# mLSTM block: the o and z projection slots cut into halves between the steps of the four heads, gating on VectorE, both token sets in one matmul

## The reference, cut to what matters

```python
xm, o_pre, z = split(hmod @ w_in, 3)              # 1024 -> 3 x 2048, latent and context tokens
xconv = silu(depthwise_conv3x3(xm) + conv_b)
q = xconv @ w_q ; k = (xconv @ w_k) * 512 ** -0.5 # per head, 4 heads of 512
v = xm
li, lf = gates(q, k, v)                           # per head and direction
# two directions r, context tokens first, their state carried into the latent tokens:
#   scores = (q k^T) * exp(decay of the forget gates + input gate - running maximum)
#   h_r    = scores v / max(|sum(scores)|, exp(-maximum))
hn = normalise(h_0 + h_1) * ln_w                  # mean and variance over the 512 of a head
y  = (sigmoid(o_pre) * hn + skip * xconv) * silu(z)
x  = x + g * (y @ w_out)                          # latent tokens only: o_pre, z, w_out see 256 tokens
```

## Time and profile before

| | |
|---|---|
| median of 3 runs | 1388.94 us (1386.91 to 1389.7) |
| the profiled execution | 1390.78 us, span 1388.9 us |
| mean granted TensorE clock | 0.961 of full speed |
| TensorE busy | 1269.3 us, 91% of the span |
| VectorE, ScalarE, GpSimd busy | 804.8, 577.3, 259.9 us |

### The profile page before, as it was taken

How to read it: one execution, slowest core, us unless ns; L and a number is a source line. 1 busy time by engine, 2 the same in 40 slices (tenths; PEclk the granted TensorE clock), 3 DMA queues, 4 the chain that set the end, 5 groups by cost and what they waited for, 6 DMA issues and landing times.

```text
span 1388.9 us, 23065 instructions
## 1 busy us (share of the span) xinstructions
PE 1269.3 (91%) x9496; PEld 1178.6 (85%) x9496; DVE 804.8 (58%) x1182; ACT 577.3 (42%) x874; POOL 259.9 (19%) x198
## 2 busy tenths in 40 slices
PE   5799999999976789899998998999989968999997
PEld 2699877779954579899998988999989957999996
DVE  2767844436446577654436676555456996555544
ACT  3332433334532313444235445444345555544433
POOL 1233300045430011000200040111001972111100
PEclk9799999999988899999999999999999989999999
DMA  9556211115530004455133534555543304355551
GB/s 390 219 211 265 98 61 61 61 61 182 182 121 1 0 31 168 158 183 184 48 122 124 185 146 145 185 182 183 184 152 122 122 31 152 124 183 182 183 190 47
DMA packets 27473, 195.56 MB, mean 141 GB/s; under 512 B 3192, under 2 KB 3328, under 8 KB 3968
## 3 DMA queue, kind: packets, MB, share of 16 engines
q1 hardware_dynamic: 26496, 191.90, 38.6%
q10 hardware_dynamic: 896, 2.50, 0.5%
HBM read 193.33 MB, written 1.05 MB: 140 GB/s over the span
## 4 chain that ended last, share of the span: by engine, by line
PE 79%; DVE 13%; ACT 4%; issue 1%; POOL 0%; ACTq 0%; DVEq 0%
PE ps L401 23%; PE ps L403 23%; PE ps L402 23%; PE ps L443 3%; PE ps L608 3%; DVE acc L1908 3%; DVE w_lo L1406 1%; PE ps L540 1%; DVE V L1647 1%; PE ps L458 1%; DVE xconv L1512 1%; DVE rstd L1717 1%; ACT w_hi L859 1%; DVE wexp L1650 1%; PE ps L596 1%
## 5 line engine op out<-in xcount | busy, mean ns | idle before, releaser
L1406 DVE TENSOR_TENSOR w_lo<-ring,w_hi 128x1024 fp32r<-128x1024 f32 x288 | 359.1, 1257 | 330.5 <-ACT w_hi L859 325.3
L859 ACT ACTIVATE w_hi<-ring 128x1024 fp32r<-128x1024 f32 x312 | 327.0, 1058 | 491.2 <-PE ps L403 412.0
L401 PE MATMUL ps<-x_hi,w_hi 128*128 128x256 f32 x1216 | 349.8, 288 | 20.2 <-DVE x_lo L1726 20.2
L402 PE MATMUL ps<-x_lo,w_hi 128*128 128x256 f32 x1216 | 348.6, 287 | 0.0
L403 PE MATMUL ps<-x_hi,w_lo 128*128 128x256 f32 x1216 | 348.4, 286 | 0.0
L401 PEld LDWEIGHTS ps<-x_hi,w_hi 128*128 128x128 f32 x1216 | 238.0, 196 | 22.5 <-issue 22.5
L402 PEld LDWEIGHTS ps<-x_lo,w_hi 128*128 128x128 f32 x1216 | 237.9, 196 | 0.0
L403 PEld LDWEIGHTS ps<-x_hi,w_lo 128*128 128x128 f32 x1216 | 237.7, 196 | 0.0
L401 PE MATMUL ps<-g_hi,w_hi 128*128 128x256 f32 x608 | 171.0, 281 | 2.5 <-POOL g_lo L1350 1.1
L403 PE MATMUL ps<-g_hi,w_lo 128*128 128x256 f32 x608 | 170.2, 280 | 0.0
L402 PE MATMUL ps<-g_lo,w_hi 128*128 128x256 f32 x608 | 169.4, 279 | 0.0
(11 more groups left out here) (299 smaller groups left out, 2157.7 us busy)
## 6 DMA issues: line engine op xcount, KB each, us to landing
ring<-in_weights SPq DMA_DIRECT2D x156, 1024.0 KB, 4.9
o_sb<-in_weights SPq DMA_DIRECT2D x10, 1024.0 KB, 6.5
z_sb<-in_weights SPq DMA_DIRECT2D x10, 1024.0 KB, 7.0
V<-in_weights SPq DMA_DIRECT2D x3, 1024.0 KB, 22.6
dft<-in_dft ACTq DMA_DIRECT2D x1, 1026.0 KB, 5.1
X<-in_x SPq DMA_DIRECT2D x1, 1024.0 KB, 4.9
ctx_room<-in_ctx SPq DMA_DIRECT2D x1, 1024.0 KB, 7.7
xconv<-in_weights SPq DMA_DIRECT2D x1, 1024.0 KB, 27.2
```

What stands on the lines that cost most here:

```text
L401: mm(dst, w_h, x_h, start=start, stop=False, skip_group_check=True)
L402: mm(dst, w_h, x_l, start=False, stop=False, skip_group_check=True)
L859: do(w_hi[:, q % 2, part], ring[:, q % RING, part], ACT.Copy).then_inc(S("hi_ready"), 1)
L1406: v.tensor_tensor(w_lo[:, q % 2, part], ring[:, q % RING, part], w_hi[:, q % 2, part], ALU.subtract).then_inc(S("lo_ready"), 1)
```

## The change

1. **Both token sets side by side.** `hc` and `hl` become one tensor `h`, and each pair of `triple`s of 256 columns in `xm_slot` becomes one of 512 columns.
2. **The order.** The oz slots are reordered by head (`block_of`: o, o, z, z for every half head), and TensorE's list is written in halves of slots: 11 halves stand before the denominators of head 0 and six with each head, at fixed places; three mout halves are among those of head 3 and 13 behind it. Each head now completes before the next one's denominators. The oz slots use two PSUM banks instead of four. ScalarE's and VectorE's queues are rewritten to the same pattern.
3. **Gating.** GpSimd keeps only memsets here. `apply_z` on VectorE multiplies o and xconv by ln_w or skip and by z, in one instruction for each chunk of 128 channels (32 in all); `rest_of_y` moves to VectorE; the rounding of y moves from VectorE to ScalarE (`round_y`).
4. **Homes.** z has two buffers in free rows of `V` instead of a tensor; `wexp` no longer shares with `hl`; the remainder of y lies in rows of `V` whose head is done. `spread` reads 128 partitions, of which 124 are zero, instead of 4; GpSimd clears them first. The loads of the oz slots are written out one by one.

```diff
+    if STARTS["oz"] <= q < STARTS["mout"]:
+        t = q - STARTS["oz"]
+        q = STARTS["oz"] + 2 * (t // 4) + t % 2 + N_OZ // 2 * (t % 4 // 2)
...
-        hc, qk_hi, room = one_place("room", (P, KE, CTX), ("hc", (P, 2, KD, CTX), F32R),
-                                    ("qk_hi", (P, 2 * HC, TOK), F32R))
-
-        hl, wexp2 = one_place("wexp", (P, 2, 2, 4, SEQ), ("hl", (P, 2, KD, SEQ), F32R))
+        both_stack = ExitStack()
+        h = tensors(both_stack)("h", (P, 2, 2, KD, SEQ), F32R)
+        both_stack.close()
+        hc, hl = h[:, 0], h[:, 1]
+        qk_hi, room = one_place("room", (P, KE, CTX), ("qk_hi", (P, 2 * HC, TOK), F32R))
+        sa("hl_room", (P, KE, SEQ))
...
-        y_lo, qk_lo, z_sb = one_place("z_sb", (P, KE, SEQ), ("y_lo", (P, KE, SEQ), F32R),
-                                      ("qk_lo", (P, 2 * HC, TOK), F32R))
-        V = sa("V", (P, HC + KE, TOK))
+        ada_room, qk_lo, wexp2 = one_place("wexp", (P, 2, 2, 4, SEQ), ("ada_room", (P, KE, SEQ), F32),
+                                           ("qk_lo", (P, 2 * HC, TOK), F32R))
+        y_rest, V = one_place("V", (P, HC + KE, TOK), ("y_rest", (P, HC + KE, TOK), F32R))
...
+        z_sb = [V[:, KE + n, :].rearrange("p (b j) -> p b j", b=2) for n in range(2)]
+
+        def y_lo(c):
+
+            return y_rest[:, HC * (c // HC) + c % HC // 2, (c % 2) * SEQ:(c % 2 + 1) * SEQ]
...
-            load_rest(first_rest, STARTS["mout"])
+            load_rest(first_rest, STARTS["oz"])
+            for q in range(STARTS["oz"], STARTS["mout"]):
+                load(q)
...
-                            triple(ps[:, bank, 0:CTX], w, [hc[:, a, k, :] for a in range(2)], k == 0, False)
-                            last = triple(ps[:, bank, CTX:TOK], w, [hl[:, a, k, :] for a in range(2)], False,
-                                          k == KD - 1)
+                            last = triple(ps[:, bank, :].rearrange("p (t j) -> p t j", t=2), w,
+                                          [h[:, :, a, k, :] for a in range(2)], k == 0, k == KD - 1)
...
+            pe.wait_ge(S("v_moved"), 4 * HEADS)
             for g in range(4):
-                if g == 2:
-                    pe.wait_ge(S("scores_moved"), HEADS)
-                last = mm(ps[0:4, (6, 7, 4, 5)[g], :], gate_fold[:, 4 * g:4 * g + 4], gates, start=True, stop=True)
+                last = mm(ps[0:4, g, :], gate_fold[:, 4 * g:4 * g + 4], gates, start=True, stop=True)
...
+            def oz_half(t, half):
+
+                if half == 0 and t >= 2:
+                    pe.wait_ge(S("oz_moved"), t - 1)
+                pe.wait_ge(S("lo_ready"), 2 * (STARTS["oz"] + t) + half + 1)
+                for k in range(4 * half, 4 * half + 4):
+                    for b in range(2):
+                        last = triple(ps[:, 6 + t % 2, b * SEQ:(b + 1) * SEQ],
+                                      [w[:, t % 2, k, b * P:(b + 1) * P] for w in wide_tiles],
+                                      [hl[:, a, k, :] for a in range(2)], k == 0 and b == 0, k == KD - 1)
+                last.then_inc(S("slot_done") if half else S("half_used"), 1)
+
+            def mout_half(t, half):
+
+                c = 2 * t + half
+                if t == 0 and half == 0:
+                    pe.wait_ge(S("oz_moved"), N_OZ)
+                    pe.wait_ge(S("heads_moved"), HEADS - 1)
+                pe.wait_ge(S("lo_ready"), 2 * (STARTS["mout"] + t) + half + 1)
+                pe.wait_ge(S("y_ready"), c // HC + 1)
+                for m in range(KD):
+                    last = triple(acc[:, m, :], [w[:, t % 2, half, m * P:(m + 1) * P] for w in deep_tiles],
+                                  (y_hi[:, c, :], y_lo(c)), c == 0 and m % 2 == 0, half == 1)
+                    if t == N_MOUT - 1 and half == 1 and m in (1, 3, 5):
+                        last.then_inc(S("bank_summed"), 1)
+                last.then_inc(S("slot_done") if half else S("half_used"), 1)
+
+            def halves(a, z):
+
+                for n in range(a, z):
+                    if n < 2 * N_OZ:
+                        oz_half(n // 2, n % 2)
+                    else:
+                        mout_half((n - 2 * N_OZ) // 2, n % 2)
+
...
             def spread(hd):
 
                 if hd:
                     pe.wait_ge(S("diag_ready"), hd)
                     pe.wait_ge(S("wexp_ready"), hd)
-                sel = cc("select", hd * P, (hd + 1) * P)[0:HEADS]
-                mm(ps[:, 0, :], sel, grow(2)[:, 0], start=True, stop=True)
-                mm(ps[:, 1, :], sel, grow(3)[:, 0], start=True, stop=True).then_inc(S("spread_done"), 1)
+                else:
+                    pe.wait_ge(S("floor_ready"), 1)
...
+                sel = cc("select", hd * P, (hd + 1) * P)
+                mm(ps[:, 0, :], sel, room[:, 4:6, :], start=True, stop=True)
+                mm(ps[:, 1, :], sel, room[:, 6:8, :], start=True, stop=True).then_inc(S("spread_done"), 1)
...
+            halves(0, 7)
+            columns()
+            halves(7, 8)
+            spread(0)
+            halves(8, 11)
             for n in range(HEADS):
-                if n >= 1:
-                    denominators(n - 1)
-                spread(n)
-                if n >= 2:
-                    head_mean(n - 2)
-                if n >= 1:
-                    mix_values(n - 1)
-                if n >= 2:
-                    head_var(n - 2)
-
-            denominators(HEADS - 1)
-            head_mean(HEADS - 2)
-            out_slots(0, 1)
-            mix_values(HEADS - 1)
-            head_var(HEADS - 2)
-            out_slots(1, 2)
-            head_mean(HEADS - 1)
-            out_slots(2, 3)
-            head_var(HEADS - 1)
...
+                at = 11 + 6 * n
+                denominators(n)
+                halves(at, at + 3)
+                if n + 1 < HEADS:
+                    spread(n + 1)
+                mix_values(n)
+                halves(at + 3, at + 4)
+                head_mean(n)
+                halves(at + 4, at + 6)
+                head_var(n)
+            halves(11 + 6 * HEADS, 2 * (N_OZ + N_MOUT))
 
             def norm(name, centred, n=KD, weight=ones_d, src=X, sqs=sq):
...
+            def move_oz(t):
+
                 act.wait_ge(S("slot_done"), STARTS["oz"] + t + 1)
-                dst = (o_sb if t < 8 else z_sb)[:, 2 * (t % 8):2 * (t % 8) + 2, :]
-                do(dst, ps[:, u, :].rearrange("p (b j) -> p b j", b=2), ACT.Sigmoid if t < 8 else ACT.Silu)\
+                n = 2 * (t // 4) + t % 2
+                if t % 4 >= 2 and n >= 2:
+                    act.wait_ge(S("z_applied"), 4 * (n - 1))
+                dst = o_sb[:, 2 * n:2 * n + 2, :] if t % 4 < 2 else z_sb[n % 2]
+                do(dst, ps[:, 6 + t % 2, :].rearrange("p (b j) -> p b j", b=2), ACT.Sigmoid if t % 4 < 2 else ACT.Silu)\
                     .then_inc(S("oz_moved"), 1)
 
+            def next_slot(t):
+
                 hi(STARTS["oz"] + t + 2)
-                move_oz(t, t % 4)
-                if t == N_OZ // 2:
-                    act.wait_ge(S("m_ready"), 1)
-                    do(grow(3)[:, 0], grow(3)[:, 0], ACT.Exp, scale=-1.0).then_inc(S("floor_ready"), 1)
+                if t < N_OZ:
+                    move_oz(t)
 
...
+            def round_y(hd):
+
+                act.wait_ge(S("head_scaled"), hd + 1)
+                do(y_hi[:, HC * hd:HC * hd + HC, :], work(2 * (hd % 2)), ACT.Copy).then_inc(S("y_rounded"), 1)
+
+            for t in range(3):
+                next_slot(t)
+            act.wait_ge(S("m_ready"), 1)
+            do(grow(3)[:, 0], grow(3)[:, 0], ACT.Exp, scale=-1.0).then_inc(S("floor_ready"), 1)
+            next_slot(3)
+            weigh(0)
+            next_slot(4)
             for n in range(HEADS):
-                weigh(n)
...
+                next_slot(5 + 3 * n)
+                next_slot(6 + 3 * n)
+                if n + 1 < HEADS:
+                    weigh(n + 1)
+                move_values(n)
+                if n:
+                    round_y(n - 1)
+                squares(n)
+                next_slot(7 + 3 * n)
+                root(n)
+            next_slot(N_OZ + 1)
+            round_y(HEADS - 1)
...
+            pool.wait_ge(S("scores_done"), HEADS)
+            nc.gpsimd.memset(room[:, 4:8, :], 0.0).then_inc(S("spread_clear"), 1)
...
-            pool.wait_ge(S("slot_done"), STARTS["oz"])
-            pool.wait_ge(S("vec_ready"), 16)
...
-            for t in range(N_OZ // 2):
-                pool.wait_ge(S("oz_moved"), t + 1)
-                for c in (2 * t, 2 * t + 1):
-                    nc.gpsimd.tensor_scalar(o_sb[:, c, :], o_sb[:, c, :], vcol("ln_w", c), None, ALU.mult)\
-                        .then_inc(S("o_scaled"), 1)
-            for t in range(N_OZ // 2):
-                pool.wait_ge(S("oz_moved"), N_OZ // 2 + t + 1)
-                pool.wait_ge(S("o_scaled"), 2 * t + 2)
-                pool.wait_ge(S("skip_ready"), 2 * t + 2)
-                c = slice(2 * t, 2 * t + 2)
```

(77 more changed lines are left out.)

62 lines of the change are left out of this document (15 added, 47 removed).

## The result

| | before | changed |
|---|---|---|
| median | 1388.47 us (4 runs, 1386.91 to 1389.7) | 1341.9 us (4 runs, 1338.37 to 1343.18) |
| ratio, 95% interval | | 0.9657, 0.9643 to 0.9671 |
| profiled execution: span | 1388.9 us | 1339.9 us |
| granted TensorE clock | 0.961 | 0.971 |

The kernel became 46.6 us faster; 1337 was forecast, with 1331 to 1352 as the range. The page of the changed kernel answers the earlier trace rows: TensorE's share of the chain that ended last has grown from 79% to 82%, and VectorE's has shrunk from 13% to 10%.

The account below looks back on a forecast made before the run. TensorE bounds it, through idling and slow clock. The stage saves 48.8 us, with xm 52.6: from 1390.8 to 1338.2, 1.8 lower for the median, 1336.4, plus half a microsecond: 1337, range 1331 to 1352.

Parts of the forecast that it names:

- the stage, grow rows to the end of mout: Oz slots, heads and mout: 204.6 us of TensorE work plus 3.8 of waits, 208.4 instead of 257.2.
- waits in it: TensorE's remaining waits in the stage: 3.0 us in the first oz slots, up to 0.6 at head 0, 0.2 in mout.
- division to values: margin for heads 1 and 3: VectorE needs 8.4 us between denominators and values; TensorE has 10.4 of other work, 8.64 for the last head.
- values to mean: margin: Between values and mean ScalarE moves 1024 elements, about 1.1 us, under one half slot of 2.88: margin 1.6.
- merged matmul, to the grow rows: Xm slots 1 to 6: 288 pairs save 13.3 ns each, 3.8 us; bounds 0 and 4.5.
- rival 2: The clock doesn't recover: fine-grained waits keep TensorE at 1.2 GHz in the values, giving back 15 us, 1352; chance 0.06.
- VectorE as the bound: VectorE's list takes 20% longer than summed, a head 36.7 us instead of 32.8, 15.6 more in all, 1353; chance 0.15.
- The clock not recovering: TensorE stays at 1.2 GHz in the values because of fine-grained waits; 15 us back, 1352; chance 0.06.
- Queues locking: In-order queues: one late item stops slots and heads alike, half the stage's gain lost, 24 us, 1361; chance 0.04.
- slower: Scattered plain float32 matmuls bring the clock down for the slots too; all at half clock 1541; chance 0.02.
- no effect: Something else keeps the heads behind the oz slots, so the change doesn't do what it says; chance 0.01.
- the half microsecond that I had added: Allowance for small handovers, half a microsecond added to 1336.4 us to give 1337.

Follow-up runs that it names:

- lo_first: Changed kernel with VectorE's splits of oz slots 2 and 3 ahead of the first scan and of g; 1339.45 us.
- before_fillers: Kernel before, with 4, 4, 5 and 8 unused matmuls ahead of the wait of mix_values of heads 0 to 3; 1387.17 us, ratio 0.9987.
- two_triples: Changed kernel with the xm slots' pair as two matmuls of 256 columns again; 1342.47 us.
- four_rows: Changed kernel with the spread over 4 rows instead of 128, as in the kernel before; 1342.26 us.
- more_tables: Changed kernel with ScalarE loading the table of Sqrt behind the move of every oz slot from the fifth on; 1338.33 us.
- order_undone: Changed kernel with only the order undone: all oz slots, columns, then heads two deep, y's rounding on VectorE, its rest on GpSimd; 1386.71 us, ratio 0.9982.
- late_slack: Changed kernel with an unused 128x512 reciprocal on VectorE for heads 1 to 3, at the end of its list; 1341.82 us.
- late_division: Changed kernel with an unused 128x512 reciprocal on VectorE for heads 1 to 3, inside the division ahead of its two passes; 1349.62 us.
- mended: Changed kernel with splits of oz slots 2 and 3 first, unused matmuls in the norms and two ahead of the first qk_lo wait; 1328.37 us, ratio 0.9561.

## Why the prediction was right, point by point

The forecast was 4.9 us too low, 0.4% of the time, on the right side and by the mechanism named. What it had wrong is the merged matmul, counted whole to the end, and the clock behind TensorE's waits of about 2 us, which it put at nothing. Term by term:

| term | predicted | measured |
|---|---|---|
| the stage, grow rows to the end of mout | 208.4 us | 209.35 |
| waits in it | 3.8 | 2.6 |
| distance from head to head | 32.8 | 32.75 |
| VectorE's work for one head, with eight gating products | 30.6 | 29.7 (head 2) |
| VectorE busy in the stage | 165 | 158.4 |
| division to values: margin for heads 1 and 3 | 1.7 and 0 | 1.68 and 0.05 |
| values to mean: margin | 1.6 | 1.6 |
| table loads in the stage; ScalarE busy | 21 (8 and 13 more); 118 us | 23 (10 before, 13 more); 117.5 us |
| merged matmul, to the grow rows | 3.8 | 1.4 (3.1 in the traces in which the clock held) |
| the norm behind mout | unchanged | 1.8 longer |

- **The order** held in all its parts. The stage is 0.95 us over the sum although the waits are 1.2 less, so 2.15 us are something else. Behind the wait of 2.2 us, eighteen matmuls of oz slot 2 take 3.66 us (313.64 to 317.30) instead of 2.16, 1.5 us, which I had not counted; the last 0.65 is not placed. lo_first shows it: without that wait the stretch is at 1.00. But the same wait, 2.24 to 2.39 us, left the clock at 1.00 in four traces (the kernel before, before_fillers, two_triples, four_rows), and lowered it in seven. My argument against rival 2, that the clock was 1.00 in the oz run with its waits, rested on one of the four. VectorE's 29.7 are the 32.75 between the divisions of heads 2 and 3 less 3.04 of waiting. I had taken w_lo at 1.2 a half, where it is 2.27 for two in a row (415.80 to 418.07), and the four masks at 1.6 where they took 1.03. For head 1, with four gating products, it is 28.1. w_lo has lost its slow passes next to GpSimd, as expected; the group answers the earlier trace rows:

```profile
L1421 DVE TENSOR_TENSOR w_lo<-ring,w_hi 128x1024 fp32r<-128x1024 f32 x46 | 54.3, 1220 | 12.3 <-ACT w_hi L892 12.2
```

- **The merged matmul** is the term that failed. The slot became 0.60 us shorter (rows of the adaptive weights 12.97 us apart, 13.57 before), 12.5 ns a pair where I had 13.3. The Trainium skill, "TensorE: Matmul & The Clock Gate", section "Back-to-back issue gap", would have made it 2.5 ns by its gap of an isolated matmul; the trace does not agree. The step that failed is "slots 1 to 6 save 288 x 13.3 ns = 3.8 us" taken whole to the end, by way of "That run begins 3.8 us earlier and is no shorter". Two things took from it.

  First, VectorE. ScalarE's move behind slot 6 comes 3.65 us earlier after the mark (78.87 instead of 82.52), but VectorE's first split comes only 2.1 us earlier (82.03 instead of 84.13). Before, VectorE had stood idle for 4.50 us ahead of it. Now it is still in the convolution, whose last two passes take 5.12 us instead of 0.88, while GpSimd's two w_lo passes run. Before, and then now:

```profile
139.99 0.88 DVE L1521 SCALAR_TENSOR_TENSOR xconv<-V,vec,xconv  x2 [0.15 <-DVE xconv L1512]
145.36 3.31 DVE L1528 TENSOR_TENSOR xsplit<-xconv,xsplit 128x512 fp32r<-128x512 f32 x4 [4.50 <-ACT xsplit L953]
```

```profile
136.93 5.12 DVE L1536 SCALAR_TENSOR_TENSOR xconv<-V,vec,xconv  x2 [0.15 <-DVE xconv L1527]
141.98 2.48 DVE L1543 TENSOR_TENSOR xsplit<-xconv,xsplit 128x512 fp32r<-128x512 f32 x4
136.84 4.93 POOL L1338 TENSOR_TENSOR w_lo<-ring,w_hi 128x1024 fp32r<-128x1024 f32 x2 [7.62 <-ACT w_hi L892]
```

  That GpSimd's passes cause it is my reading of the times and was not tested by itself. Over six xm slots VectorE is busy 66.0 us of 77.8, where it was 58.0 of 81.5. The splits themselves are 0.9 us quicker, so q of head 0 is released 2.95 us earlier (107.08 instead of 110.03 us after the mark). two_triples, with the old matmuls, has the first split at 84.12 and the release at 110.01 again.

  Second, the clock. TensorE gained 4.2 us over seven slots and waits 2.2 us for the release instead of 0.9. Behind that wait the stretch of the qk slots takes 12.77 us at a clock of 0.87. In the kernel before it took 11.19 at 1.00:

```profile
171.26:182.45 11.19, 11.19 (x50) 9.24 (x51) 6.19 (x9) 4.41 (x8) 0.00 (x0) 1.00 0.28 96
```

  So in this trace 1.6 of the 2.95 us are given back, and 1.4 stay. In four_rows and more_tables, where the clock held, 3.1 stay.
- **The rest of the program** was taken as unchanged, and the norm behind mout was not. The same instructions after almost the same wait took 5.41 us in seven of the traces with 1.90 to 1.98 us of waiting and 3.72 in two; the two traces with 1.83 (the kernel before and order_undone) had 3.72. What decides between them is not settled here. The fastest of the changed kernel's own runs (1338.37 us) had a mean clock of 0.976 and the other three 0.971 or 0.972, so part of the spread of one kernel is the clock. The Trainium skill, "TensorE: Matmul & The Clock Gate", section "What's actually happening", says that the same kernel shows different numbers of slow matmuls from run to run, by the phase in which the clock gate happens to look. The traces agree so far: the same instructions after nearly equal waits were slow in some and not in others, at this place and at the two waits of about 2 us named above.
- **The rivals.** VectorE as the bound: out as throughput (late_slack), real as latency (late_division). The clock not recovering: out in the values (7.07 to 7.17 us for 32 records), but its mechanism, idling before a low clock, is what took 1.6, 1.5 and 1.7 us of this trace elsewhere. Queues locking, slower, no effect: out by the waits. ScalarE's table loads, against which I had quoted a rule of the Trainium skill ("ScalarE: Activation LUTs", section "Table sets: the hidden batching unit"): 23 loads, and even 34, lie beside TensorE's work, and the next activation starts 0.01 us after the 1.28 us of a load (351.62 and 352.91), so its 2.7 us a switch do not show here.
- **The base.** I took 1.8 us off for the distance of the profiled execution of before from its median. The changed kernel's stood at its median, so 1.8 of the 4.9 us are that; 1.3 us from slot 0 went the other way. Sum: 2.4 (merge) + 1.8 (norm) + 0.95 (stage) - 0.2 (rest) - 1.3 (slot 0) = 3.6 for the profiled execution, and 1.8 less the half microsecond that I had added. Slot 0 and the base are chance, in opposite directions. The lower bound has a slip: 3.8 and 0.7 below 1337 is 1332.5, not 1331; nothing hangs on it.

## What to carry to other kernels

When a matrix engine waits in turn with a vector engine, lay fixed pieces of independent matrix work between each step and its answer, and check each gap by latency (answer time against cover), not by the engines' busy shares: here 8.4 us of division under 10.4 us of cover gave away nothing, and 3.35 us more inside it in each of three heads cost 7.7 us in all, but nothing by the median at the end of the list. When one engine's work is made faster, look at what its neighbours now do at the same time, and at the wait that follows: here passes of VectorE fell beside those of GpSimd, and the longer wait lowered the clock in most traces, so that 1.4 to 3.1 us were left of 3.6. Look for waits of 2 to 5 us with slow matmuls behind them; a few matmuls without a use in such waits, in all the norms, were worth 8.6 us here, at no cost to the result.

## What the runs showed of the hardware that was not expected

- Waits of TensorE of 0.90 us (two_triples, the kernel before) and of 1.23 and 1.35 us (late_division, before_fillers) left the granted clock at 1.00; those of 2.95 us and more ahead of the values did not. Between them it went either way with the same instructions: waits of 1.84 to 2.24 us in the qk slots were followed by a low clock in seven traces of nine, 2.24 to 2.39 us ahead of oz slot 2 in seven of eleven, and 1.83 to 1.98 us ahead of the variance behind mout in seven of eleven. Each fall there took 1.5 to 1.7 us. In four_rows the clock fell with TensorE busy all the time, behind a spread over 4 rows. In the kernel before it fell during such a spread, after a wait of only 1.14 us (0.57 over 399.7 to 403.2 us).
- Two VectorE passes of 128x255 that take 0.88 us together took 5.12 us while GpSimd ran two passes of 128x1024 (4.93 us). In xm, single passes of the convolution above 2.5 us (otherwise about 0.5) appear seven or eight times in the traces of the changed kernel, of order_undone and of mended, and once in each of the kernel before, two_triples and before_fillers. That the two engines hold each other up is read from these times; no run tests it alone.
- Seven loads of ScalarE's tables in a head (more_tables, head 1) cost nothing that reached TensorE: 1283 ns each, 34 of them in 209 us.
- The length of the first xm slot differs by up to 3 us between traces in which its instructions are the same or do the same work (the mark behind it lies from 58.4 to 61.4 us), which is more than several effects studied here. Comparing traces from a mark behind such a stretch, instead of from their start, is what made the effect of the merge readable.
